# A fused transformer block and expert layer in float32: the later modulation products move from TensorE to VectorE

## The reference, cut to what matters

```python
m  = (jax.nn.silu(c)     @ w_ada[l] + b_ada[l]).reshape(b, 1, N_MOD, d)   # 9 vectors of 1024
mc = (jax.nn.silu(c_ctx) @ w_ada[l] + b_ada[l]).reshape(1, 1, N_MOD, d)
x  = x + 0.5 * m[:, :, 2] * swiglu(modulate(rmsnorm(x, norm_ffn1[l]), m[:, :, 0], m[:, :, 1]), w_ffn1_in[l], w_ffn1_out[l])
...
mod   = (jax.nn.silu(c) @ w_mod + b_mod)[:, None, :]                      # second block: 6 vectors of 1024
mod_c = (jax.nn.silu(c_ctx) @ w_mod + b_mod)[None, None, :]
```

## Time and profile before

| what | value |
|---|---|
| median of 3 runs | 3545.49 us (3538.64 to 3547.33) |
| the profiled execution | 3544.62 us, of which 3542.8 us are the span of the profile |
| PE busy | 2950.5 us (83%) |
| DVE, ACT, POOL busy | 1370.6 us (39%), 910.4 us (26%), 1091.0 us (31%) |
| ffn1 `ffn_in` | about 83 to 517 us |
| ffn2 `ffn_in`, `ffn_out` | about 1136 to 1380 us, 1389 to 1528 us |
| expert layer | from about 2245 us to the end |

### The profile page before, as it was taken

The page is one execution under the profiler, slowest core; times in us unless marked ns, Lnnn a source line. Parts: engine busy times, 40 slices in busy tenths (PEclk is TensorE's granted clock), DMA queues, the critical chain, the costliest instruction groups (busy, mean ns, idle before and its releaser), DMA issues.

```text
span 3542.8 us, 30390 instructions
## 1 busy us (share of the span) xinstructions
PE 2950.5 (83%) x11480; PEld 1967.4 (56%) x11480; DVE 1370.6 (39%) x3163; ACT 910.4 (26%) x1596; POOL 1091.0 (31%) x731
## 2 busy tenths in 40 slices
PE   6999989987887998979956689777877777877776
PEld 4888889965335887759832568333333333333332
DVE  3000012020552002030044422666676667666764
ACT  3111122134333223232233332322222222222221
POOL 1222222223002443322310023344444444444442
PEclk8999999988799999989977699899999898988899
DMA  4444442212001223411210022899999999999996
GB/s 191 153 159 154 154 141 60 62 54 71 0 1 60 96 101 109 141 58 60 66 37 1 1 83 83 341 420 420 420 420 420 420 420 415 420 413 416 409 419 283
DMA packets 119458, 721.99 MB, mean 204 GB/s; under 512 B 14372, under 2 KB 16684, under 8 KB 45996
## 3 DMA queue, kind: packets, MB, share of 16 engines
q0 software_dynamic: 73728, 536.90, 36.7%
q1 hardware_dynamic: 37448, 127.67, 10.7%
q10 hardware_dynamic: 8164, 55.89, 4.6%
HBM read 718.31 MB, written 2.10 MB: 203 GB/s over the span
## 4 chain that ended last, share of the span: by engine, by line
PE 55%; DMA 27%; DVE 10%; ACT 4%; issue 2%; POOL 1%; SPq 0%; ACTq 0%; DVEq 0%; POOLq 0%
PE acc L495 12%; PE acc L496 12%; PE acc L497 12%; PE acc L895 10%; DMA hid<-in_peer_rows,squares 9%; DMA resid<-in_peer_rows,squares 7%; DMA wring<-in_peer_rows,squares 4%; DMA wring<-in_w_ffn_in 2%; PE sums L439 2%; DMA modw<-in_w_ada 2%; PE misc L439 2%; DVE hid L1385 1%; PE misc L466 1%; DVE hid_parts L1391 1%; DMA modw<-in_w_mod 1%
## 5 line engine op out<-in xcount | busy, mean ns | idle before, releaser
L1976 POOL TENSOR_TENSOR wring_parts<-wring,wring_parts 128x1024 fp32r<-128x1024 f32 (+1 forms) x215 | 506.4, 2368 | 1665.2 <-ACT wring_parts L916 1665.2
L495 PE MATMUL acc<-hid_parts,wring_parts 128*128 128x384 f32 (+1 forms) x2128 | 787.7, 370 | 80.2 <-DVE hid_parts L1391 62.7
L497 PE MATMUL acc<-hid_parts,wring_parts 128*128 128x384 f32 (+1 forms) x2128 | 770.9, 362 | 0.0
L496 PE MATMUL acc<-hid_parts,wring_parts 128*128 128x384 f32 (+2 forms) x1696 | 615.7, 363 | 0.0
L495 PEld LDWEIGHTS acc<-hid_parts,wring_parts 128*128 128x128 f32 x2128 | 403.9, 190 | 184.4 <-issue 108.3
L895 PE MATMUL acc<-wring,squares 128*128 128x512 f32 x688 | 346.3, 662 | 111.0 <-ACT squares L916 111.0
L497 PEld LDWEIGHTS acc<-hid_parts,wring_parts 128*128 128x128 f32 x2128 | 404.7, 190 | 38.3
L916 ACT ACTIVATE wring_parts<-wring 128x1024 fp32r<-128x1024 f32 (+1 forms) x215 | 222.2, 1040 | 624.3 <-DMA wring<-in_w_ffn_out 232.3
L496 PEld LDWEIGHTS acc<-hid_parts,wring_parts 128*128 128x128 f32 (+1 forms) x1696 | 323.5, 191 | 28.4
L895 PEld LDWEIGHTS acc<-wring,squares 128*128 128x128 f32 x688 | 142.4, 212 | 313.3 <-issue 193.9
L916 ACT ACTIVATE hid<-hid 128x4 f32<-128x4 f32 (+2 forms) x164 | 39.9, 243 | 955.5 <-DVE hid L1876 317.4
(11 more groups left out here) (271 smaller groups left out, 3464.0 us busy)
## 6 DMA issues: line engine op xcount, KB each, us to landing
wring<-in_w_ffn_in SPq DMA_DIRECT2D x88, 512.0 KB, 4.2
modw<-in_w_ada ACTq DMA_DIRECT2D x28, 1024.0 KB, 5.3
modw<-in_w_mod ACTq DMA_DIRECT2D x24, 1024.0 KB, 5.3
wring<-in_w_ffn_out SPq DMA_DIRECT2D x32, 512.0 KB, 3.5
wring<-in_w_in SPq DMA_DIRECT2D x28, 512.0 KB, 3.3
wring<-in_w_mix_in SPq DMA_DIRECT2D x18, 512.0 KB, 3.3
wring<-in_peer_w_q SPq DMA_DIRECT2D x16, 512.0 KB, 3.3
hid<-in_w_ada SPq DMA_DIRECT2D x6, 1024.0 KB, 18.5
```

What stands on the lines that cost most here:

```text
L495: nc.tensor.matmul(o, wh, high, start=first, stop=False)
L496: nc.tensor.matmul(o, wh, low, start=False, stop=False)
L497: return nc.tensor.matmul(o, wl, high, start=False, stop=last)
L1976: nc.gpsimd.tensor_tensor(Wlor[:, p, 0:blocks, 0:cols], Wlo[:, p, 0:blocks, 0:cols], Whir[:, p, 0:blocks, 0:cols], ALU.subtract).then_inc( ...
```

## The change

The later 26 groups go in 13 pairs. DVE now multiplies: a quarter is two blocks of k of one group (`Mw` is now two buffers of 512 KB), and for each block and each of the two conditions one instruction multiplies the 128 x 512 block by the condition's column and adds it to a running sum, which lies in one of four tiles (`mod_sums`: two groups x two conditions). The first block of a group is only multiplied (tensor_scalar), the other seven are multiplied and added (scalar_tensor_tensor). Two quarters stand behind each unit's multiplication with the silu. After a pair's 8 quarters PE sums the four tiles over partitions with a matrix of ones (`mod_add`, four matmuls), DVE copies the bank, and `mod_turn_pair` turns both groups with four small matmuls. 10 pairs are done in ffn1's `ffn_in`, 3 in ffn2's `ffn_in`, none in ffn2's `ffn_out`.

```diff
-            def mod_later(half, group, blk, landed, first=False, stage=0):
...
-                pe.wait_ge(mod_loaded, landed)
-                mod_half(misc, Mw, blk, half)
+            def mod_add(pairs):
+                pe.wait_ge(mod_used, pairs * QUARTERS)
+                for j in range(4):
+                    mm = nc.tensor.matmul(misc[32 * j:32 * j + 2, :], ones[:, 0:2], mod_sums[j], start=True, stop=True, skip_group_check=True)
+                mm.then_inc(mod_half_done, 1)
+
+            def mod_turn_pair(pair, count):
+                pe.wait_ge(modrows_ready, count)
+                for t in range(4):
+                    mm = nc.tensor.matmul(mod_ps[:, :].rearrange("p (g t c) -> p g t c", t=4, c=2)[:, ds(pair * 2 + FIRST_GROUPS, 2), t, :],
+                                          modrows[:, t * P:(t + 1) * P], c_("sel_pair").rearrange("p (g c) -> p g c", g=2), start=True, stop=True)
+                mm.then_inc(mod_turned, 1)
...
-                        if mods:
-                            mod_later(q % 2, i * 2 + (FIRST_GROUPS + q // 2), blk, i * 64 + 16 * (q + 1), isinstance(i, int) and q == 0, 1 if isinstance(i, int) else 0)
+                        if halves == 2 and not (isinstance(i, int) and i == 0):
+                            if q == 0:
+                                mod_add(i)
+                            if q == 1:
+                                mod_turn_pair(i - 1, i + FIRST_GROUPS)
+                        u = i * units + q if halves == 1 else 0
+                        if halves == 1 and u in (4, 8, 12):
+                            mod_add(EARLY_PAIRS + u // 4)
+                        if halves == 1 and u in (5, 9, 13):
+                            mod_turn_pair(EARLY_PAIRS + u // 4 - 1, FIRST_GROUPS + EARLY_PAIRS + u // 4)
...
-                if c == 2:
-                    half = IN_HALVES + j
-                    mod_later(half % 2, half // 2, 1, 16 * (half - FIRST_HALVES + 1), first=j == 0)
...
+            def mod_load(x):
+                if x >= 2:
+                    act.wait_ge(mod_used, x - 1)
+                group = FIRST_GROUPS + x // 4
+                w, group = (a["w_ada"], group) if group < ADA_GROUPS else (a["w_mod_2"], group - ADA_GROUPS)
+                act.dma_start(Mw[:, x % 2, :, :], w[group].rearrange("p (q k n) -> p q k n", q=4, k=2)[:, x % 4, :, :]).then_inc(mod_loaded[x % 2], 16)
...
+                for u in range(units * FT // 2):
+                    act.wait_ge(acc_ready, base + u + 1)
+                    run(sg[:, (base + u) % 2, 0:width], acc[:, 2 * ((base + u) % 2), 0:width], ACT.Silu).then_inc(silu_ready, 1)
+                    if u % halves == halves - 1:
+                        for m in range(2):
+                            high_part(s0 + W_RING + 2 * (u // halves) + m)
+                    for x in range(first_quarter + 2 * u + 2, min(first_quarter + 2 * u + 4, stop_quarter)):
+                        mod_load(x)
...
+            def mod_quarter(x):
+                pair, group, kq = x // QUARTERS, FIRST_GROUPS + x // 4, x % 4
+                blk = 0 if group < ADA_GROUPS else 1
+                dve.wait_ge(mod_loaded[x % 2], 16 * (x // 2 + 1))
+                for k in range(2):
+                    for c in range(2):
+                        o, col = mod_sums[x // 4 % 2 * 2 + c], cnd[:, blk, 2 * kq + k, c:c + 1]
+                        if k == 0 and kq == 0:
+                            ins = V.tensor_scalar(o, Mw[:, x % 2, k, :], col, None, ALU.mult)
+                        else:
+                            if k == 1:
+                                dve.wait_ge(mod_step, 3 * x + 1 + c)
+                            elif c == 0:
+                                dve.wait_ge(mod_step, 3 * x)
+                            else:
+                                dve.wait_ge(mod_used, x)
+                            ins = V.scalar_tensor_tensor(o, Mw[:, x % 2, k, :], col, o, ALU.mult, ALU.add)
+                        ins.then_inc(mod_used if k == 1 and c == 1 else mod_step, 1)
...
+                for u in range(2 * sides * FT // 2):
+                    f, hf = u // sides, u % sides
+                    dve.wait_ge(silu_ready, done + u + 1)
+                    free(V.tensor_tensor(arena[:, (f * sides + hf) * width:(f * sides + hf + 1) * width], sg[:, (base + u) % 2, 0:width],
+                                         acc[:, 2 * ((base + u) % 2) + 1, 0:width], ALU.mult), base + u)
+                    pair = first_pair + u // 4
+                    if u % 4 == 0 and first_pair < pair <= stop_pair:
+                        mod_rows_of_pair(pair - 1)
+                    if pair < stop_pair:
+                        mod_quarter(pair * QUARTERS + u % 4 * 2)
+                        mod_quarter(pair * QUARTERS + u % 4 * 2 + 1)
```

More of the change, by code:

```diff
@@ L530, in _, with ffn_in @@
             mod_turn(FIRST_GROUPS - 1)
[L532 removed]
+            def ffn_in(name, width, halves, h_before):
                 units = 2 * halves
@@ L1171, in _ @@
             shift(2, hi512r, lo512, 6 * KD, T, 2)
-            silus("ffn2_in", T, 1)
+            for x in range(2):
+                mod_load(EARLY_PAIRS * QUARTERS + x)
+            silus("ffn2_in", T, 1, EARLY_PAIRS * QUARTERS, N_PAIRS_OF_GROUPS * QUARTERS)
             ff_parts("ffn2_out", UNIT["ffn2_in"], ff512, hi_ff512)
-            stat(KD, T, lambda j: behind_chunks_and_group("ffn2_out", j, T))
+            stat(KD, T, lambda j: behind_chunks("ffn2_out", j, T))
             def renormed(j):
@@ L1418, in mod_rows, with mod_rows_of_pair @@
                 V.tensor_copy(modrows[:, :], source).then_inc(modrows_ready, 1)
-            def swiglu(name, width, sides, done, mods=False):
-                units, base = 2 * sides, UNIT[name]
-                def step(i):
-                    for q in range(units):
-                        u0 = base + q
-                        sub, hf = q // sides, q % sides
-                        dve.wait_ge(silu_ready, i * units + (done + q + 1))
-                        free(V.tensor_tensor(arena[:, ds(i * 2 * width * sides + (sub * sides + hf) * width, width)],
-                                             sg[:, u0 % 2, 0:width], acc[:, 2 * (u0 % 2) + 1, 0:width], ALU.mult), u0)
-                        if mods and q % 2 == 1:
-                            mod_rows(misc[:, :], i * 2 + (FIRST_GROUPS + q // 2))
-                step(0)
-                with dve.Fori(1, FT // 2) as i:
-                    step(i)
+            def mod_rows_of_pair(pair):
+                dve.wait_ge(mod_half_done, FIRST_HALVES + pair + 1)
+                dve.wait_ge(mod_turned, FIRST_GROUPS + pair)
+                V.tensor_copy(modrows[:, :], misc[:, :]).then_inc(modrows_ready, 1)
@@ L1448, in ff_parts, with residual @@
                     ins.then_inc(ff_ready, 1)
-            def residual(name, sides, ffn, mods=False):
+            def residual(name, sides, ffn):
                 for j in range(KD):
```

115 lines of the change are left out of this document (35 added, 80 removed).

## The result

The changed kernel takes 3458.39 us (median of 4 runs, 3458.22 to 3461.35), the one before in the same comparison 3542.12 us (3538.64 to 3547.33): ratio 0.9761, 95% interval 0.9749 to 0.9774, 83.7 us less. The forecast was 3517 us, the range 3490 to 3548. The direction was right, the time was not. The traced execution took 3461.35 us; its rows follow.

A forecast was written before the change was run, and what follows sets the result against it. PE was taken to set the pace in ffn1's first product. PE savings of -57.5 us, +25 for waits and +4 in ffn2 gave -28.5: 3544.6 to 3516.1, as a median 3517 us, range 3490 to 3548.

The forecast's parts named there:

- The prices of PE: PE in ffn1's first product: 8.35 us per unit of 48 matmuls, 1.18 per sum, 1.06 per turn alone.
- PE in ffn2's second product, -12.0: Eight halves and four turns leave PE's queue in ffn2's second product, saving 12.0 us.
- I take 2.5 us per pair ... +25: ffn1's first product: PE waits at each sum for DVE, delayed by POOL; 10 pairs, +25 us, bounds +7 and +37.
- 512 KB more cost 1.1 us in landing, so weights and quarter both come up to 1.1 us late: Loads in ffn1's first product: 5.3 us for 1 MB against 4.2 for 512 KB, so both land up to 1.1 late.
- rival C: Slower, about 3573 us, chance 0.08: waits at upper bound, each followed by PE at 1.2 GHz, 3 us per slow stretch.
- DVE in ffn2's first product, +4: DVE and POOL work outlasts ffn2's first-product units, adding 4 us over 12 units, bounds 0 and +9.
- The loop sum of 11.9 us: ffn2's first product: silu, multiplication, eight DVE instructions, POOL and load issue total 11.9 us per unit, against 11.4 available.
- The rest costs nothing: ACT's extra issue, unrolled code of DVE, ACT and PE, and DVE's bank copy were priced at 0 us.
- A: No wait, 3488 us, chance 0.11: DVE keeps the ports through its eight instructions, POOL works afterwards, PE never waits.
- D: DVE at half its rate, 1.37 us per instruction, about 3820 us (some +275), chance 0.01.

The follow-up runs named there:

- the first two experiments: Kernel before with four unused columns in its constants table, 3518.39 us; kernel before with only the constants' SBUF tile four columns wider, 3517.78 us.

## Why the prediction was off

**The prices of PE held.** The silus of the changed kernel stand 8.32 us apart, 9.49 over a sum and 9.25 over a turn: a unit costs 8.32 (forecast 8.35), a sum 1.17 (1.18), a turn 0.93 (1.06). 43 x 8.32 + 10 x 1.17 + 10 x 0.93 = 378.8 us, where the forecast had 381.5 without waits. "PE in ffn2's second product, -12.0": from ffn2's last silu to the first transpose behind the product it is 151.8 us before and 138.9 after, -12.9. The -14.1 of the table are over a longer stretch, whose rest scatters by some 7 us among kernels with the same instructions there (803.9 to 810.7 for the whole stretch in those of the changed order). Three pairs in ffn2's first product cost 7.0 us, forecast 6.7 without waits. For all of the change without a new wait the forecast had -57.5; the runs gave -62.6 and -60.0 at equal starts.

**"I take 2.5 us per pair ... +25" is the first step that failed.** The changed kernel has no such wait. The collision of POOL with DVE's last instructions is a real mechanism, for the experiment without loads shows it, but the moment of POOL's start, which the forecast fed into it, is wrong. That the experiment costs 25.3 us and the forecast had 25 is partly luck: the waits sum to 19.7 us (2.4 each instead of 2.5, and 0.3 in two), and some 5 us are the slow stretches that the forecast left to rival C. The step "512 KB more cost 1.1 us in landing, so weights and quarter both come up to 1.1 us late" mis-sized the delay. It compared two transfers of different size, and in the kernel before no load of `modw` was under way while a weight tile was. In the changed kernel they overlap, and the tiles of ffn1 land 2.0 us later (6.0 instead of 4.0): ACT's high part starts 5.81 us behind the silu with the quarters and 3.65 without, 2.2 us later. POOL then begins 6.6 to 7.5 us behind the silu in the ten units ahead of a sum, and DVE is done at 6.38 (in four of the ten it is 0.1 to 0.9 later, and in two of these POOL starts 0.1 and 0.4 us before its last instruction ends, which holds up neither the sum nor a tile). The forecast also had DVE 0.3 us too late, by 0.685 instead of 0.66 an instruction and a start at 1.2 instead of 1.0. The delay that it feared removed the collision.

**"DVE in ffn2's first product, +4" failed in the same direction.** DVE and POOL do take turns there as forecast. Timelines of POOL, DVE and PE in the unit ahead of the first sum:

```profile
1137.40 5.45 POOL L1981 TENSOR_TENSOR wring_parts<-wring,wring_parts 128x1024 fp32r<-128x1024 f32 x2 [5.30 <-ACT wring_parts L922]
...
1137.71 2.88 DVE L1427 SCALAR_TENSOR_TENSOR squares<-modw,cond,squares 128x512 f32<-128x512 f32 x1
1140.52 2.88 DVE L1427 SCALAR_TENSOR_TENSOR arena<-modw,cond,arena 128x512 f32<-128x512 f32 x1
...
1143.45 0.59 PE L485 MATMUL misc<-tmp,cst 128*2 128x512 f32 x1
```

But DVE ends at 1143.40, 10.90 us behind the silu, and PE starts the sum at 10.95, after a pause of 0.1 us: the unit is just long enough. The loop sum of 11.9 us had put both of POOL's instructions and all eight of DVE's one after the other in every unit; in three of the twelve units two of DVE's instructions are held up, in six one, and in three none, since there POOL comes within the last one or behind it. For three pairs in this product the forecast had +10.7 in all, and 7.0 were measured. (In ffn1 of the changed kernel the exclusive lock, which the Trainium skill states in "SBUF — State Buffer", section "SBUF: two separate sides", cost PE nothing; where the engines met, here and without the loads, the rows shown agree with it.)

**"The rest costs nothing" is the second step that failed**, and the largest single miss together with the wait. It did not look at the table of constants at all. Four columns moved every buffer behind it from a start at 32 bytes past a multiple of 64 to a multiple of 128, and the gathers of the expert layer, bound by DMA at a share of 1.01, ran at 427 instead of 420 GB/s: 24 us.

**The rivals.** A had nearly the right time without the shift (3488 against 3480.3) for the wrong reason: POOL is not held off until DVE is through, it gets in at the first boundary (4.79 and 2.89 us above); it only came too late to meet it. (The row of tensor_tensor in the earlier trace rows, on which A rests, ran on with three more instructions to 545.67, and POOL ended at 547.92, 2.3 us behind it: a row of that kind did hold POOL off.) C's slow stretch is real, 3 of 10 waits in the kernel without loads, but each was worth 1.6 us, and the changed kernel has no such waits. D fell: 0.66 us an instruction. 3517 less the wait (25), ffn2 (4) and the start (24) is 3464; of the remaining 6 us the units' 0.03 and the turns' 0.13 together make 2.7 (381.5 against 378.8), ffn2's second product makes 0.9, and the rest lies in stretches that scatter. The last stretch, 40.3 to 40.4 us in the three kernels of the old order and 35.3 to 39.2 in those of the new, I leave open, and so the 3.3 us more ahead of ffn2, where two kernels with the same instructions (the first two experiments) differ by 4.9.

## What to carry to other kernels

A constant or a small buffer that is added at the front of SBUF is part of the change: where a later stage is full of DMA, look at the start of the buffers it writes, and measure a change against a kernel with the same layout, or its gain is credited to the wrong edit. A wait that is forecast from the order of three engines hangs on tenths of a microsecond: price what an added transfer does to the ones beside it from a place where both are under way, since one that delays the trigger of a collision can remove the collision. The reverse holds for what comes after: this kernel's sums are free only because POOL is late, and a change that makes the weight tiles land 2 us earlier costs it 25 us.

## What the runs showed of the hardware

Gathers into SBUF are sensitive to the start of the destination: 420 GB/s at 32 bytes past a multiple of 64, 421 at an odd multiple of 64, 427 at a multiple of 128, with the DMA engines full in each case; worth 19 to 25 us of 3.5 ms, nearly all of it in a stretch of 1.2 ms. A DVE scalar_tensor_tensor of 128 x 512 with a column as scalar that meets a POOL tensor_tensor of 128 x 1024 lasts 2.8 to 2.9 us instead of 0.74, and the two engines alternate instruction by instruction. A pause of PE of 2.4 us was followed by a stretch at the lower granted clock in three cases of eight, though PE had been busy without a gap for more than 30 us ahead of each; each of the three cost 1.6 us. The four pauses of 2.3 to 5.5 us at the sums of the kernels with half the turns were all followed by such a stretch.
